# Output pieces of a state-space group as high and low halves, and one set of exponents moved

## What is computed

```python
y = y_diag + y_off + x * d_skip.reshape(G, R)[..., None]
...
y = y * jax.nn.silu(z.astype(f32))
yg = y.reshape(bsz, seqlen, N_GROUPS, D_INNER // N_GROUPS)
yg = yg * lax.rsqrt(jnp.mean(yg * yg, axis=-1, keepdims=True) + RMS_EPS)
y = (yg.reshape(bsz, seqlen, D_INNER) * norm_g.astype(f32)).astype(z.dtype)
return y @ out_w
```

## Time and profile before

| | us |
|---|---|
| median of 3 runs | 914.5 (913.82 to 914.9) |
| profiled execution | 914.06 |
| its span | 912.0 |
| PE busy in the span | 899.6 (99%) |
| DVE busy | 736.4 (81%) |
| ACT busy | 580.8 (64%) |

### The profile page before, as it was taken

How to read it: one execution, slowest core, us unless ns; L and a number is a source line. 1 busy time by engine, 2 the same in 40 slices (tenths; PEclk the granted TensorE clock), 3 DMA queues, 4 the chain that set the end, 5 groups by cost and what they waited for, 6 DMA issues and landing times.

```text
span 912.0 us, 18311 instructions
## 1 busy us (share of the span) xinstructions
PE 899.6 (99%) x6623; PEld 847.9 (93%) x6623; DVE 736.4 (81%) x1361; ACT 580.8 (64%) x998; POOL 38.0 (4%) x50
## 2 busy tenths in 40 slices
PE   9999899999999999999999999999999999999997
PEld 7999899999999999998888888999999999999886
DVE  5999698889889988689888646889979988888543
ACT  5649677887877575556666535579656766666332
POOL 1000110110110000000000000100000000000000
PEclk9999999999999999999999999999999999999999
DMA  8577478888876537447655555455447455555601
GB/s 330 182 267 230 133 172 251 224 224 241 206 218 222 208 119 272 165 133 248 196 185 184 189 189 167 138 177 190 152 134 253 152 202 178 181 179 177 230 1 47
DMA packets 48510, 172.04 MB, mean 189 GB/s; under 512 B 5668, under 2 KB 6344, under 8 KB 48328
## 3 DMA queue, kind: packets, MB, share of 16 engines
q1 hardware_dynamic: 43488, 154.74, 51.0%
q0 software_dynamic: 2880, 10.49, 6.0%
q10 hardware_dynamic: 2088, 6.08, 1.8%
HBM read 159.72 MB, written 1.09 MB: 176 GB/s over the span
## 4 chain that ended last, share of the span: by engine, by line
PE 66%; issue 24%; DVE 6%; ACT 2%; DMA 1%; POOL 1%; SPq 0%; POOLq 0%; DVEq 0%; ACTq 0%
PE A L472 10%; PE A L473 10%; PE A L474 10%; PE B L696 6%; PE A L504 4%; PE B L504 3%; PE B L472 2%; PE B L473 2%; PE B L474 2%; PE A L506 2%; DVE w_lo L1396 2%; PE B L506 2%; PE B L777 2%; PE A L777 1%; PE A L485 1%
## 5 line engine op out<-in xcount | busy, mean ns | idle before, releaser
L1396 DVE TENSOR_TENSOR w_lo<-raw,w_hi 128x1024 fp32r<-128x1024 f32 x249 | 301.7, 1219 | 75.9 <-ACT w_hi L930 75.3
L930 ACT ACTIVATE w_hi<-raw 128x1024 fp32r<-128x1024 f32 x249 | 259.4, 1051 | 72.0 <-PE A L778 20.9
L472 PE MATMUL A<-h,w_hi 128*128 128x256 f32 x952 | 274.7, 289 | 2.9 <-ACT gates L1094 2.8
L474 PE MATMUL A<-h,w_lo 128*128 128x256 f32 x952 | 269.3, 283 | 0.0
L473 PE MATMUL A<-h,w_hi 128*128 128x256 f32 x952 | 269.3, 283 | 0.0
L472 PEld LDWEIGHTS A<-h,w_hi 128*128 128x128 f32 x952 | 182.1, 191 | 6.3 <-issue 5.5
L473 PEld LDWEIGHTS A<-h,w_hi 128*128 128x128 f32 x952 | 182.3, 192 | 0.3
L474 PEld LDWEIGHTS A<-h,w_lo 128*128 128x128 f32 x952 | 182.2, 191 | 0.0
L472 PE MATMUL B<-h,w_hi 128*128 128x256 f32 x352 | 100.1, 285 | 0.0
L473 PE MATMUL B<-h,w_hi 128*128 128x256 f32 x352 | 99.6, 283 | 0.0
L474 PE MATMUL B<-h,w_lo 128*128 128x256 f32 x352 | 99.6, 283 | 0.0
(11 more groups left out here) (313 smaller groups left out, 1634.9 us busy)
## 6 DMA issues: line engine op xcount, KB each, us to landing
raw<-in_weights_dram SPq DMA_DIRECT2D x289, 512.0 KB, 4.3
w_lo<-raw POOLq DMA_DIRECT2D x20, 512.0 KB, 4.7
csrow<-cs_dram ACTq DMA_DIRECT2D x9, 512.0 KB, 4.7
x<-in_x_dram SPq DMA_DIRECT2D x4, 256.0 KB, 4.6
bd<-in_lru_w_dram ACTq DMA_DIRECT2D x1, 1024.0 KB, 5.8
out_dram<-m_wide SPq DMA_DIRECT2D x3, 256.0 KB, 2.1
raw<-in_weights_dram SPq DMA_DIRECT2D x2, 256.0 KB, 5.1
par<-in_params_dram SPq DMA_DIRECT2D x1, 379.0 KB, 7.2
```

Source lines behind the costliest of these rows:

```text
L472: mm(dst, wh, lo, start=first, stop=False, skip_group_check=free)
L474: return mm(dst, wl, hi, start=False, stop=last, skip_group_check=free)
L930: F(w_hi[:, s, :], raw[:, s, :], ACT.Copy).then_inc(hi_ready, 1)
L1396: V.tensor_tensor(w_lo[:, s, :], raw[:, s, :], w_hi[:, s, :].bitcast(F32), ALU.subtract).then_inc(lo_ready, 1)
```

## The change

Both output pieces of each turn (places 2 and 6, 14 pieces in all) leave `NATIVE`: ACT and DVE split them like others, and PE makes three products per tile with `yn_hi` and `yn_lo` in place of `yn`. A new step `y_high` on ACT copies yn to yn_hi (two copies of 128 x 256), a new step `y_low` on DVE subtracts it to yn_lo. ACT does y_high of the group before near the start of a turn, behind the splits of pieces 6 and 7; DVE does y_low between the taps of b and c and the subtraction and taps of x. Two hi copies a turn are added on ACT and two subtractions on DVE, whose list `los` gets them in order, so later ones move back by one place. The buffers share room with stage and stage2. Besides, the exponents of group 1 go from behind the drain of piece 6 of the first turn to behind piece 5's, with a wait for y_ready.

```diff
+OUT_SPLIT = (2, 6)
+NATIVE = frozenset(GLU_NATIVE) | frozenset([LOOP0 + 8 * i + n for i in range(GROUPS - 1) for n in OUT_AT
+                                            if n not in OUT_SPLIT]) | frozenset(range(TAIL0, PW0))
...
             def out_piece(p, turn, g, c, between=None):
-                native_loaded(p, turn)
-                pe.wait_ge(scale_read, g + 2)
+                split = p not in NATIVE
+                if split:
+                    pe.wait_ge(lo_ready, split_order(p, turn))
+                    pe.wait_ge(yn_low, g + 1)
+                else:
+                    native_loaded(p, turn)
+                    pe.wait_ge(scale_read, g + 2)
                 for m in range(KD):
                     if between is not None and m == KD // 2:
                         y_transposes(between)
+                    if split:
+                        at = OUT_SPLIT.index(OUT_AT[c])
+                        ins = tile(p % RING, m, yn_hi[:, at, :], yn_lo[:, at, :], acc_out(m), False, False, True)
+                        continue
...
+            def y_high(g):
+
+                act.wait_ge(scale_read, g + 2)
+                for n, at in enumerate(OUT_SPLIT):
+                    ins = F(yn_hi[:, n, :], yn[:, OUT_AT.index(at), :], ACT.Copy)
+                ins.then_inc(yn_high, 1)
...
+                if OUT_AT[1] in OUT_SPLIT:
+                    split(0)
                 split(1)
+                y_high(g - 1)
                 split(2)
...
                 drain_input(2, 2, base + IN_AT[2], t)
+                if OUT_AT[0] in OUT_SPLIT:
+                    split(4)
                 split(5)
...
-                    if n == 6:
+                    if n == 5:
+                        act.wait_ge(y_ready, 1)
                         exponents(1)
...
             g = GROUPS - 1
-            for n in range(3):
-                split_hi(GATES0 + n + LEAD)
+            split_hi(GATES0 + LEAD)
+            split_hi(GATES0 + 1 + LEAD)
+            y_high(g - 1)
+            split_hi(GATES0 + 2 + LEAD)
...
+            def y_low(g):
+
+                dve.wait_ge(yn_high, g + 1)
+                for n, at in enumerate(OUT_SPLIT):
+                    ins = V.tensor_tensor(yn_lo[:, n, :], yn[:, OUT_AT.index(at), :], yn_hi[:, n, :].bitcast(F32),
+                                          ALU.subtract)
+                ins.then_inc(yn_low, 1)
...
                     conv_inputs(g, (0, 1))
+                    y_low(g - 1)
                     lo()
                     conv_inputs(g, (2, 3))
```

More of the change, by code:

```diff
@@ L78 @@
 GLU_NATIVE = (0, 1, 2, 3, 9)
-NATIVE = frozenset(GLU_NATIVE) | frozenset([LOOP0 + 8 * i + n for i in range(GROUPS - 1) for n in OUT_AT]) | frozenset(range(TAIL0, PW0))
+OUT_SPLIT = (2, 6)
+NATIVE = frozenset(GLU_NATIVE) | frozenset([LOOP0 + 8 * i + n for i in range(GROUPS - 1) for n in OUT_AT
+                                            if n not in OUT_SPLIT]) | frozenset(range(TAIL0, PW0))
 LOW_AT = (1, 4, 7)
@@ L131, in split_order @@
 def split_order(p, turn=0):
-    return sum(q not in NATIVE and q not in LOW for q in range(p)) + 1 + (6 - len(LOW_AT) if p < GATES0 else 8) * turn
+    return sum(q not in NATIVE and q not in LOW for q in range(p)) + 1 + (6 + len(OUT_SPLIT) - len(LOW_AT) if p < GATES0 else 8) * turn
 def low_turn(p):
@@ L190, in hybrid_kernel @@
         scale = sb("scale", [P, TT])
+        s0 = ExitStack()
+        yn_hi = sb("yn_hi", [P, 2, T], F32R, s0)
+        yn_lo = sb("yn_lo", [P, 2, T], F32R, s0)
+        s0.close()
         stage = sb("stage", [P, 2, T])
@@ L351, in hybrid_kernel @@
         yt_ready, first_tap = sem("yt_ready"), sem("first_tap")
+        yn_high, yn_low = sem("yn_high"), sem("yn_low")
         conv_operand_ready, mixed_ready = sem("conv_operand_ready"), sem("mixed_ready")
```

## The result

The changed kernel takes 927.62 us in the median of four runs (926.54 to 929.23), the kernel before 914.57 (four runs). The ratio is 1.0147, with a 95% interval of 1.0135 to 1.0159: 13 us slower. The forecast was 922.0, with a range to 927.5. The direction and the mechanism that it named are there; what is missing is 5.6 us, and nearly all of it has one cause.

What follows compares the result with a forecast made beforehand. PE was taken to bound the kernel at 27.59 us a turn. The sum -2.8 + 5 x (29.2 - 27.6) + 1.55 + 1.13 - 0.33 = +7.6 us on 914.06 gave 921.7, forecast as 922.0, range 914.5 to 927.5.

Steps and rivals of the forecast that it cites:

- the mechanism: In looped turns y_high ends late on ACT; DVE waits 1.9 us for it and PE about 2.7 for yn_lo.
- The ring without clock: Hand-overs through PE, ACT and DVE from one turn's decayed scores to the next: 29.2 us a turn against 27.59.
- so I charge no clock: PE's idle of 2.78 us in the first turn left its clock at 1.00, so no slowdown was added.
- to group 1: First turn, up to the decayed scores of group 1: a gain of 2.8 us.
- five looped turns: Middle turns of the group loop, each 29.2 us against 27.6: 5 x (29.2 - 27.6), +8.0 us.
- last turn: Piece 7 is split in one step there, DVE waits 0.85 us: 29.15 us against 27.6, a loss of 1.55.
- the subtraction behind it: One more DVE subtraction ahead of conv_sum_ready in the last turn, costing 1.13 us.
- The slack of 0.33: In the last turn PE's wait for conv_sum_ready ended 0.33 us after it came; this was taken off the loss.
- The exponents' move: First turn: 4.0 us leave the stretch that PE waited on, PE's wait of 2.78 goes; gain 2.8 us.
- Rival (a): ACT isn't late, y_high is ready when DVE comes; DVE sets 27.3 us a turn, 911.5; chance 0.13 shared with another rival.
- Rival (c): Every new hand-over costs and ACT's splits and csrow issue stretch under earlier weight loads: 30.2 us a turn, 928; chance 0.12.
- the waits for weights: ACT's waits before the y squares, 4.2 us a turn, should go, since split slots are free at their subtraction.

Runs made afterwards that it cites:

- e3: Changed kernel with y_high as ACT's first step, ahead of the splits of pieces 6 and 7, in the loop and last turn: 912.24 us, ratio 0.9973.
- e4: Changed kernel with ten matmuls of zeros on PE in front of its wait for yn_lo at the first output piece: 920.89 us, ratio 1.0067.
- e7: Changed kernel with five matmuls of zeros on PE in front of the first output piece's wait: 920.76 us, ratio 1.0060.
- e1: Kernel before, with only the exponents of group 1 moved ahead in the first turn: 910.11 us, ratio 0.9949.
- e8: Changed kernel with y_low on DVE behind piece 6's subtraction instead of in front of it: 930.86 us, ratio 1.0168.
- e2: Changed kernel with the exponents of group 1 back at their old place: 933.27 us, ratio 1.0198.

## Why the prediction was right and wrong

- Direction and mechanism held. y_high behind two splits is late, DVE stands for it and PE for yn_lo: forecast 1.9 and 2.7 us, measured 1.98 and 2.6. e3 moves it by two splits and takes the whole loss back.
- The ring without clock was right: 29.2 forecast, 29.1 in e4 and e7.
- The step that failed is "so I charge no clock": the ring held no term for a slower output piece. I had one gap of 2.78 us on PE in the trace after which the clock stayed at 1.00, and took it for all. In the changed kernel the gaps of 2.56 to 2.62 us, one in each of five looped turns, were each followed by a lower clock on the 24 matmuls behind. That costs 1.55 us on the piece and the same in the turn, because in this order of work the scores come behind the piece on PE and DVE is already there. Five turns at 30.70 in place of 29.2 are 7.5 us, which is what the profiled run lies above the 921.7 of my sum; the misses of the other terms, below, cancel.
- Terms against the profiled run: to group 1, 2.8 forecast and 2.5 to 2.8 measured (122.80 and 93.27 against 125.33 and 92.97); five looped turns +8.0 forecast, 153.51 - 137.85 = +15.7 measured; last turn +1.55 forecast, 28.64 - 27.74 = +0.9 measured (29.2 less the 1.05 of one split step would be 28.15, so the 29.15 of my text has a 1.0 in it that it doesn't name; the trace has it, as 11.4 us from y_low to M where a looped turn of e4 takes 10.5); the subtraction behind it +1.13 forecast and measured (331.08 - 304.95 = 26.13 against 25.00). The slack of 0.33 in front of conv_sum_ready gave nothing in the end: PE waited 0.95 us there, and the whole delay of 15.2 us went through. Sum -2.5 + 15.7 + 0.9 + 1.1 = 15.2.
- The exponents' move was mis-sized when alone: 4.0 us in the first turn and not 2.8, since the late ACT also held DVE's next subtraction, and with it the next turn's scores (5.73 us of wait, 1.70 in e1).
- Rival (a), no wait for y_high, is what e3 makes true by another order; the turn is then 27.69 (ACT's ring) and not my 27.3. Rival (c) had the right size (a turn over 30, 928) by the wrong cause: hand-overs and weight loads cost nothing beyond the sum, as the turn of 29.1 in e4 shows, and the waits for weights went, as forecast.
- The range ended at 927.5 and the median is 927.62. It would have held it if the clock had been a bound of its own. At the lower level the steps of the changed kernel's matmuls are 0.21 us in place of 0.120, so a whole output piece of 24 at that level would cost at most 2.3 us a turn; measured are 1.55.

What stays open: when the clock falls. Gaps of 1.24 to 1.66 us never lowered it, those of 2.0 did in three of five, one of 2.27 (e8) did, and those of 2.5 to 2.6 did in all sixteen looped turns that have one (the changed kernel, e2 and e8); but the gap of 2.78 us in the first turn of the kernel before, and of e2 too, did not. Ahead of both kinds of gap PE ran split products of h at 0.120 us a step. Also open is the spread of the changed kernel's times, 926.5 to 929.2: it would fit one or two turns without the fall in the faster ones, but only one of the runs has its trace here.

## What to carry to other kernels

A step that crosses engines (here: yn to ACT, to DVE, to PE) should be placed by following the ring from its producer to its consumer, counting every instruction queued ahead of it on each engine. Two splits ahead of 0.7 us of copies turned a change that could be even into 13 us of loss, and one moved line gave it back. Even so both pieces split gain nothing (912.2 against 910.1 for the exponents alone), while the one at place 2 by itself, with y_high first, gains 3.5 us (906.6): in a loop like this, split only as much as the other engines have room for. When a forecast leaves PE a gap that comes back every turn, price a lower clock for the work behind it, even if one gap of that length in the trace was harmless.

## What the runs showed of the hardware

- Behind an idle of 2.0 to 2.6 us PE may run the next 4.4 us at a granted clock of 0.62 to 0.67 (a mix of 2.4 and 1.2 GHz), and 24 matmuls then take 4.45 us for 2.89. The fall comes around PE's restart (in e2 at the end of the wait, in the changed kernel 0.9 us behind it, with PE busy). With 2.0 us of idle the same loop showed it in some turns and not in others.
- Matmuls of zeros in the gap, five of 512 columns, were enough to keep the clock at 1.00 with 1.3 us of idle left: 6.9 us of the 13 came back by doing more work. Two were not enough (928.1).
- A tile of 256 columns takes 0.432 us as a plain fp32 product and 3 x 0.120 = 0.360 us as three split ones, in the kernel before; the output piece of e4, eight tiles in 2.89 us, has the same 0.120.
